# Encoder layer with attention, convolution and experts on one core: x tiles over two queues, convolution parts in place, a new list order, router products behind the last chunk

## What is computed

```python
h = rms_norm(x, norm1_g)
u = h @ w_in                                   # 1024 x 2560
q, k, v, uc = split(u)                         # 3 x 512, 1024
a = neighbourhood_attention(q, k, v, rpb)      # 8 heads x 64
c = conformer_conv(uc)                         # GLU, depthwise conv of width 31, layer norm, swish
x = x + concat(rms_norm(a), rms_norm(c)) @ w_out
h = rms_norm(x, norm2_g)
x = x + hier_moe(h)                            # top group of 4, then top 2 of its 8 experts
y = rms_norm(x, final_g)
```

## Time and profile before

| what | us |
|---|---|
| median of 3 runs | 912.96 |
| lowest, highest | 912.54, 914.18 |
| the profiled execution's own time | 913.56 |
| its span, first to last instruction | 911.7 |

### The profile page before, as it was taken

One profiled execution on the slowest core, in us unless ns is written; L12 is line 12 of the kernel. 1 busy time (PEld: TensorE's weight loads), 2 busy tenths in 40 slices (PEclk: granted clock), 3 DMA queues, 4 the chain that ended last, 5 costly groups with the idle time before them and its releaser, 6 DMA issues.

```text
span 911.7 us, 15694 instructions
## 1 busy us (share of the span) xinstructions
PE 848.1 (93%) x5814; PEld 571.5 (63%) x5815; DVE 374.4 (41%) x697; ACT 242.3 (27%) x482; POOL 139.2 (15%) x288
## 2 busy tenths in 40 slices
PE   3989999999979999989999879999999999999984
PEld 2879977777757878965555445555555555555531
DVE  5399979796374535541111101111111111111146
ACT  5223216545675222101111111111111111111122
POOL 4200010000000001022222111212222212121113
PEclk9998999999979999899999999999999999999997
DMA  7543543413251293959999999999999999999975
GB/s 210 125 91 104 156 162 139 151 47 105 66 166 47 104 401 147 402 214 418 423 418 420 419 419 422 418 420 420 420 420 419 420 420 420 419 414 420 391 290 185
DMA packets 82014, 266.04 MB, mean 292 GB/s; under 512 B 19129, under 2 KB 44985, under 8 KB 57401
## 3 DMA queue, kind: packets, MB, share of 16 engines
q1 hardware_dynamic: 64272, 245.11, 68.9%
q0 software_dynamic: 7888, 18.78, 5.4%
q10 hardware_dynamic: 9816, 1.66, 1.0%
HBM read 247.53 MB, written 27.34 MB: 302 GB/s over the span
## 4 chain that ended last, share of the span: by engine, by line
PE 55%; DMA 16%; SPq 7%; DVE 6%; issue 1%; ACT 1%; POOL 0%; POOLq 0%; DVEq 0%; ACTq 0%
DMA big<-in_w_up 16%; PE ps L1299 14%; PE ps L1336 9%; PE ps L1053 8%; PE ps L1186 7%; SPq L771 7%; PE ps L1302 3%; PE ps L1314 2%; DVE big L1713 2%; PE ps L1290 2%; PE ps L1072 2%; PE ps L1105 1%; PE ps L1084 1%; PE ps L690 1%; PE ps L1205 1%
## 5 line engine op out<-in xcount | busy, mean ns | idle before, releaser
L2026 DVE TENSOR_TENSOR big<-ps,big 64x256 f32<-64x256 f32 x78 | 33.2, 426 | 392.0 <-ACT big L1592 392.0
L1302 PE MATMUL ps<-ring,big 128*64 128x256 f32 x704 | 156.1, 379 | 4.7 <-DMA ring<-in_w_up 4.7
L1299 PE MATMUL ps<-ring,big 128*64 128x256 f32 x704 | 156.4, 379 | 0.9 <-DVE big L2015 0.9
L1053 PE MATMUL ps<-hT,w_split 128*128 128x512 f32 (+1 forms) x768 | 145.7, 345 | 4.1 <-DVE hT L1651 3.6
L1053 PEld LDWEIGHTS ps<-hT,w_split 128*128 128x128 f32 x768 | 118.6, 191 | 26.2 <-issue 11.7
L1299 PEld LDWEIGHTS ps<-ring,big 128*64 128x64 f32 x704 | 96.0, 137 | 56.3 <-issue 12.5
L1302 PE MATMUL ps<-big 128*64 128x256 f32 x544 | 121.5, 380 | 5.1 <-DMA big<-in_w_up 5.1
L1299 PE MATMUL ps<-big 128*64 128x256 f32 x544 | 121.6, 380 | 0.0
L1302 PEld LDWEIGHTS ps<-ring,big 128*64 128x64 f32 x704 | 96.1, 137 | 10.5 <-DMA ring<-in_w_up 6.4
L1299 PEld LDWEIGHTS ps<-big 128*64 128x64 f32 x544 | 73.9, 137 | 39.2 <-issue 9.0
L1592 ACT ACTIVATE big<-ps 64x256 f32<-64x256 f32 x78 | 29.3, 375 | 245.1 <-PE ps L1302 231.7
(11 more groups left out here) (244 smaller groups left out, 1092.5 us busy)
## 6 DMA issues: line engine op xcount, KB each, us to landing
ring<-in_w_gate SPq DMA_DIRECT2D x44, 1024.0 KB, 27.3
ring<-in_w_up SPq DMA_DIRECT2D x44, 1024.0 KB, 28.0
ring<-in_w_down SPq DMA_DIRECT2D x44, 1024.0 KB
big<-in_w_gate SPq DMA_DIRECT2D x20, 1024.0 KB
big<-in_w_up SPq DMA_DIRECT2D x20, 1024.0 KB
big<-in_w_down SPq DMA_DIRECT2D x20, 1024.0 KB
w_raw<-in_w_in SPq DMA_DIRECT2D x20, 512.0 KB, 4.1
results<-spare POOLq DMA_DIRECT2D x12, 512.0 KB, 2.9
```

The source lines that it names most:

```text
L1053: mm = pe.matmul(ps[:, n % 2, 0:size], w_split[:, sub, hi_w, k, :], hT[:, k // 4, hi_h, k % 4, cols], **flags)
L1299: pe.matmul(ps[0:BLK, 6 * h, 0:FH], xT[:, k % (KD // 2), q, :], gate_w[s][:, k, fs], start=(k == 0), stop=(k == KD - 1))
L1302: mm = pe.matmul(ps[BLK:2 * BLK, 6 * h + 1, 0:FH], xT[:, k % (KD // 2), q, :], up_w[s][:, k, fs], start=(k == 0), stop=(k == KD - 1))
L2026: nc.vector.tensor_tensor(hb[:, fs], ps[BLK:2 * BLK, 6 * h + 1, 0:FH], sG[:, fs], ALU.mult).then_inc(hb_ready[h], 1)
```

## The change

- **Start:** SyncE loads x tiles 0 and 3, n1 and the weights; ScalarE's queue loads tiles 1, 2, 4 and 5. The orders of ScalarE and VectorE over squares, scaling and parts are rewritten. The very first group is cut by columns: its first half needs h tiles 0 and 1 only.
- **Convolution parts in place:** high and low part of the convolution get buffers of their own (conv_hi, conv_lo), so they no longer wait for hT. w_out block 1 has its own raw and split buffers, too.
- **List order:** CHUNKS has conv 3 ahead of qk 0; COST, FIRST, PATIENCE are new numbers for plan().
- **Second norm and scores of the router:** the turned tiles use other banks (TURN_BANK), the router products move, fillers are fewer.
- **Rows stored once:** h_rows has half its size; row_idx holds its own indices, from one more comparison and one addition.
- **First expert round on TensorE** is written out, with the first block's register loads ahead of the wait for its rows.

```diff
-CHUNKS = [("conv", 0), ("conv", 1), ("v", 0), ("v", 1), ("conv", 2), ("qk", 0), ("conv", 3), ("qk", 1), ("qk", 2), ("qk", 3)]
+CHUNKS = [('conv', 0), ('conv', 1), ('v', 0), ('v', 1), ('conv', 2), ('conv', 3), ('qk', 0), ('qk', 1), ('qk', 2), ('qk', 3)]
...
-    return 4 if CHUNKS[c][0] != "v" and g % 2 == 0 else 2
+    return 4 if CHUNKS[c][0] != "v" and g % 2 == 0 and (c, g) != (0, 0) else 2
...
-FIRST = dict(win=50, ht=1, sc=10, tn=8, va=8, inv=7, mean=15, meanb=3, var=2, rows=0, rowsb=0, ssc=3, asum=6, poa=45, po=45, tnh=20, lgt=2,
+FIRST = dict(win=22, ht=26, sc=8, tn=5, va=14, inv=6, mean=16, meanb=16, var=19, rows=2, rowsb=18, ssc=0, asum=19, poa=23, po=23, tnh=-5, lgt=26,
...
+TURN_BANK = (4, 0, 4, 0, 4, 2)
...
-        in_line(("chi", j), [("silu", j), last_group])
+        in_line(("chi", j), [("silu", j), ("ssc",)])
...
-            after += [("alo", PAIRS - 1), ("sh", ASLOTS - 1)] if s else [("clo", JC - 1)] + [taker(*g) for g in groups[-2:]]
+            after += [("alo", PAIRS - 1), ("sh", ASLOTS - 1)] if s else [("clo", JC // 2 - 1)] + [taker(*g) for g in groups[-2:]]
...
-        in_line(("po", s), [], line="po")
+        in_line(("po", s), [] if s else [("clo", JC - 1)], line="po")
...
-    h_rows = nc.dram_tensor("h_rows", (4 * T, D // 2), F32, kind="Internal").ap()
+    h_rows = nc.dram_tensor("h_rows", (2 * T, D // 2), F32, kind="Internal").ap()
...
-            for t in range(NT):
-                sp.dma_start(x[:, t, :], rows_of(x_prompt, x_sample, t)).then_inc(x_in[t], 16)
-                if t == 0:
-                    sp.dma_start(n1, bass.AP(norm1.tensor, 0, [[0, P], [1, D]])).then_inc(n1_in, 16)
-                elif t == NTS - 1:
-                    load_win(0)
+            sp.dma_start(x[:, 0, :], rows_of(x_prompt, x_sample, 0)).then_inc(x_in[0], 16)
+            sp.dma_start(n1, bass.AP(norm1.tensor, 0, [[0, P], [1, D]])).then_inc(n1_in, 16)
+            sp.dma_start(x[:, 3, :], rows_of(x_prompt, x_sample, 3)).then_inc(x_in[3], 16)
+            load_win(0)
             load_win(1)
...
+            sp.wait_ge(osplit_done, OUT_CHUNKS - 1)
             sp.wait_ge(wout_done, NT * OUT_CHUNKS // 2)
...
             for t in range(NT):
                 sp.wait_ge(h2_ready, t + 1)
-                for j in range(2):
-                    sp.dma_start(h_whole[j * T + t * P:j * T + (t + 1) * P, :], h2[:, t, :]).then_inc(h2_out, 16)
+                sp.dma_start(h_whole[t * P:(t + 1) * P, :], h2[:, t, :]).then_inc(h2_out, 16)
...
+                if n == 0:
+
+                    pe.wait_ge(h_ready, 2 * q + 2)
+                    some = slice(2 * P * q, 2 * P * (q + 1))
+                    for k in range(KD):
+                        for m, (hi_w, hi_h) in enumerate(HI_LO):
+                            mm = pe.matmul(ps[:, 0, some], w_split[:, 0, hi_w, k, :], hT[:, k // 4, hi_h, k % 4, some],
+                                           start=(k == 0 and m == 0), stop=(k == KD - 1 and m == 2))
...
-                    if a[0] == NT - 1:
-                        pe.wait_ge(x2_done, max(g for g in range(len(OUT)) if OUT_BANK[g] == 7) + 1)
-                        stay_busy(4)
...
-            stay_busy(32)
+            pe.wait_ge(x2_done, len(OUT))
+            stay_busy(26)
             pe.wait_ge(order_ready, 1)
...
             pe.wait_ge(table_ready, 1)
+            first_blocks = blocks_of(0)
             pe.wait_ge(xb_copied, 1)
             turn_rows()
             stay_busy(3)
...
+            for t in (1, 2, 4, 5):
+                act.dma_start(x[:, t, :], rows_of(x_prompt, x_sample, t)).then_inc(x_in[t], 16)
...
             def hi_of_conv(j):
                 act.wait_ge(silu_done, j + 1)
-                nc.scalar.activation(mT[:, 0, 0, j, :], conv_out[:, j, :], ACT.Copy,
+                if j == 0:
+                    act.wait_ge(ssc_done, 1)
+                nc.scalar.activation(conv_hi[:, j, :], conv_out[:, j, :], ACT.Copy,
                                      scale=vec[:, V_GO + JC + j:V_GO + JC + j + 1]).then_inc(chi_done, 1)
...
             def lo_of_w_out(n):
                 dve.wait_ge(ohi_done, n + 1)
+                if n == 0:
+                    dve.wait_ge(win_done, len(GROUP_AT))
...
             link(V.tensor_scalar(nobody[:], ps[:, 5, 0:NB], 0.0, float(8 * T), ALU.is_equal, ALU.mult))
+            link(V.tensor_scalar(second, ps[:, 5, 0:NB], float(2 * T), float(-2 * T), ALU.is_gt, ALU.mult))
+            link(V.tensor_tensor(second, second, nobody[:], ALU.add))
```

More of the change, by code:

```diff
@@ L196, in parts @@
                 after += [taker(*groups[n - 2])] if n >= 2 else []
-            in_line(("win", c, g, q), after, COST["narrow" if kind == "v" or g % 2 else "part"], "win")
-            if n == 0 and q < 2:
-                in_line(("ht", 4 + q), [], line="win")
+            in_line(("win", c, g, q), after, COST["first" if n == 0 else "narrow" if kind == "v" or g % 2 else "part"], "win")
+            if n == 0 and q == 0:
+                for t in range(NTS, NT):
+                    in_line(("ht", t), [], line="win")
         done = ("win", c, g, parts_of(c, g) - 1)
@@ L333, in release @@
     def release(name):
-        engine, at = ENGINE[name[0]], 5.0 if name[0] == "strip" else 0.0
+        engine, at = ENGINE[name[0]], 8.0 if name[0] == "strip" else 0.0
         for d in work[name][1]:
@@ L1027, in turn_h @@
                 mm.then_inc(xps, 1)
-            for t in range(4):
+            for t in range(NTS):
                 turn_h(t)
@@ L1339, in expert_block, with blocks_of, blocks, expert @@
                 mm.then_inc(y_done, 1)
+            def blocks_of(place):
+                n = pe.value_load(table[0:1, bass.ds(place, 1)], min_val=1, max_val=MAXN)
+                first = pe.value_load(table[0:1, bass.ds(place + E, 1)], min_val=0, max_val=MAXB - 1)
+                return n, first
+            def blocks(n, first, s, target):
+                with pe.Fori(0, n) as j:
+                    expert_block(first + j, s, target)
+            def expert(place, s, target):
+                blocks(*blocks_of(place), s, target)
             pe.wait_ge(table_ready, 1)
+            first_blocks = blocks_of(0)
             pe.wait_ge(xb_copied, 1)
@@ L1344, in _ @@
             stay_busy(3)
-            def expert(place, s, target):
-                n = pe.value_load(table[0:1, bass.ds(place, 1)], min_val=1, max_val=MAXN)
-                first = pe.value_load(table[0:1, bass.ds(place + E, 1)], min_val=0, max_val=MAXB - 1)
-                with pe.Fori(0, n) as j:
-                    expert_block(first + j, s, target)
-            with pe.Fori(0, E // SLOTS) as i:
+            blocks(*first_blocks, 0, 16)
+            for place in range(1, SLOTS):
+                expert(place, place, 16)
+            with pe.Fori(1, E // SLOTS) as i:
                 for s in range(SLOTS):
@@ L1656, in lo_of_run @@
                 nc.vector.tensor_tensor(lo, w_raw[:, run % 2], fp32(hi), ALU.subtract).then_inc(split_done, 1)
-            scaled(0)
-            scaled(1)
-            for t in range(NT):
-                lo_of_h(t)
-                if t + 2 < NT:
-                    scaled(t + 2)
-                if t in (2, 4):
-                    lo_of_run(t // 2 - 1)
+            for t in range(3):
+                scaled(t)
+            lo_of_h(0)
+            scaled(3)
+            lo_of_h(1)
+            lo_of_run(0)
+            lo_of_h(2)
+            scaled(4)
+            lo_of_h(3)
+            scaled(5)
+            lo_of_run(1)
+            lo_of_h(4)
+            lo_of_h(5)
             dve.wait_ge(vec_in, 16)
```

113 lines of the change are left out of this document (63 added, 50 removed).

## The result

| | before | after |
|---|---|---|
| median, us | 912.83 (4 runs) | 903.86 (4 runs) |
| lowest, highest | 912.54, 914.18 | 901.84, 905.35 |
| the profiled execution's own time | 913.56 | 904.92 |
| its span | 911.7 | 903.1 |

The change makes the kernel 1.1% faster: the ratio is 0.9893, with a 95% interval of 0.9876 to 0.991. That is 9.0 us by the medians and 8.6 between the two profiled executions, where 15.2 were forecast.

A forecast was written before the change was run, and what follows sets the result against it. Ahead of 399 us TensorE bounds the kernel; the expert stage behind is a fixed block of some 481 us. Terms -2.5 - 7.1 - 6.9 - 1.2 + 2.5 = -15.2 us gave 897.8 us, range 890 to 907.

The forecast's parts named there:

- Term 1: At the start: reordered squares, splits and a column-cut first group bring TensorE's w_in products earlier, -2.5 us.
- Rival B: At the start: norm row and tile 3 come late, the term becomes +1, total 901.3 us; chance 0.08.
- Term 2: At the convolution's end: parts in their own place remove a stall and half clock, less new waits, -7.1 us.
- Term 3: Around the last output chunk: three of six groups of router products move behind it, at full clock, -6.9 us.
- Term 4: At the list: fewer fillers, two more VectorE operations, register loads moved ahead of the wait, -1.2 us.
- Term 5: At the first gather: weight preloads still fill the DMA engines, so the gather takes longer, +2.5 us.
- A: Before the expert stage: VectorE binds in part, its waits and half clock cost 6 us, total 904; chance 0.15.
- E: Conv-and-attention stretch: VectorE becomes its bound, the moved chunk's 28 us of taps join the path, total 926; chance 0.05.
- F: At the expert stage's start: everything won ahead is given back as a wait, total 913; chance 0.03.

The follow-up runs named there:

- experiment 4: Kernel after with all six x tiles and the norm row on SyncE's one queue, new orders kept: 903.44 us, ratio 0.9902.
- experiment 2: Kernel after with the remaining weight preloads issued behind the third stored tile instead of the sixth: 898.94 us, ratio 0.9842.
- experiment 5: Three edits of the kernel after: first, high parts wait for the last w_in group again, 902.39 us; old chunk sequence, 911.3 us; both, 909.29 us.
- experiment 6: Kernel before with only the chunk sequence changed (conv 3 ahead of qk 0), planned with its old numbers: 920.4 us, ratio 1.0057.
- experiment 8: Kernel of experiment 2 with the first three groups of router products placed late among the output products: 897.65 us, ratio 0.9826.
- experiment 7: Kernel after with the router products of the first three tiles back between the output products: 904.64 us, ratio 0.9903.
- experiment 1: Kernel after with 16 fillers instead of 4 ahead of the wait for the first gathered rows: 901.22 us, ratio 0.9869.

## Why the prediction was right, and where it was not

The forecast was 897.8 with 890 to 907; the time is 903.86, inside. The sign and the places were right; the sum was 6 us too good, and the mechanism behind its largest term was wrong for the most part. The first expert product stood at 388.66, not at 384. That the time lies inside the range owes something to the range's width: no term names what took most of the 6 us.

**Term 1 (forecast -2.5):** measured -4.2 in the profile, and 2.7 to 4.3 over the nine kernels with this start (the wait ends at 62.59 to 64.27, against 66.92). The norm row came late, as feared (VectorE's first scaling waited for it until 11.29), but TensorE begins on w_in at 21.74, and with one queue at 21.06. Rival B was right that the row lands late (9.7 us for 6.1) and wrong on the price. The rule of the Trainium skill (DMA: Bandwidth & Descriptors, Issuing engines are not separate DMA queues) that transfers started by several engines run on the same 16 DMA engines agrees with experiment 4: the gain of the two queues is nil. The estimate tied to it, -1.5 for the reordering, was too small.

**Term 2 (forecast -7.1):** the size was right where the clock held, the cause was wrong. From the wait at chunk 1 to the last output product TensorE takes 230.1 us (110.95 to 341.09), where it took 242.7 (115.75 to 358.45): 12.6 less, forecast 15.1 for terms 2 and 3 together (7.1, and 8.0 ahead of the last chunk). In the profile of experiment 2, whose clock holds in 105 to 165, it is 227.1 (111.83 to 338.91): 15.6 less. The wait for the split of w_out was 0.80 (0.5), the one at mean 2 2.37 (1.5), the one at mean 3 didn't come. But the step "After the change the convolution's parts have a place of their own and no longer wait for the last w_in group" doesn't carry the 7.1: experiment 5 puts that wait back, which costs 1.4 us up to the last output product and nothing in the total. The sequence of chunks, which the prediction had only as a cost, is worth 7.4 us in the changed kernel (experiment 5). It does not take the stretch away alone: in the kernel before, with the old numbers, stretch and half clock stay (experiment 6). So the gain belongs to the sequence together with the planner's new numbers, and the place has a small part in it.

**Term 3 (forecast -6.9):** the part ahead of the last chunk (-8.0) is in the numbers of term 2. Behind that chunk it took 16.5 us where 13.3 were forecast, against 12.2 before. The step that failed is "13.3 us from the last chunk to the last router product at full clock". The 13.3 were worked out with products at full clock, but a row of nothing but router products and turns had a mean of 0.79: 3.2 us more. The price at full clock was right: 8.04 us for half the router products in experiment 8, and three groups of 1.7 more make 13.1. The row is at 0.79 or 0.80 in six profiles, at 0.89 in the two with the wait put back, and with half as many router products at 1.00 (7 and 8).

**Term 4 (forecast -1.2):** right where the clock holds. Last router product to first order product 7.6 us for 8.5; the next steps to the gather's issue 14.6 (365.17 to 379.79) for 14.0. The 0.8 of the register loads is in experiment 2 (2.0 for 2.87), and in the kernel after it is hidden by half clock (2.97).

**Term 5 (forecast +2.5):** measured +2.9, and experiment 2 shows its cause. What the forecast lacked is what stands behind it: TensorE has fillers for a gather of 3 us, a longer one lets it stand 3.26 us, and the turn and the first block then run at half clock. In the profile 0.9 us more stand ahead of the first expert product and 1.8 behind than forecast; experiment 1's 12 fillers take away 0.95 and 1.15 of them, so 0.6 of the 2.7 is not shown to be clock.

**The sum in the profile:** -15.2, +3.2 clock in the router products, +2.7 behind the gather (2.1 of it clock), +0.4 gather, +2.5 ahead of the last chunk (mostly the half clock of that execution at the two means), -1.7 start, -0.6 between the start and chunk 1's mean (48.2 us for 48.8, in no term): -8.7, against -8.6 measured. Of the rivals, A gave the nearest number (904), and part of its mechanism was there: VectorE's waits were 1.2 us over the forecast (0.80 and 2.37 for 0.5 and 1.5), and half clock followed them in this profile. But most of the 6 us came from elsewhere. What was priced wrongly was TensorE's clock: in a row where it does not wait, and behind waits that term 5 and the two means made. E and F fell: TensorE is busy 102.64 of 105.00 us from 136.20 to 241.20, and the expert stage is 480.94 us.

## What to carry to other kernels

A transfer made longer is paid twice if the engine behind it was kept busy for the old length: once in the wait, once in the clock of the work that follows. When a stall goes away after a change of several parts, put each part back alone before naming it, and look at its stage as well as the total: here the wait put back cost 1.4 us in its stage and nothing in the total, and the sequence that the gain hung on made the old kernel slower. And spread narrow products between wide ones rather than into one row, provided that each stands where its input is long ready; here that held the clock, but its gain in time (1.3 us) is not told apart from nothing, and it moved the preloads closer to the gather.

## What the runs showed of the hardware that was not expected

- TensorE fell to its lower clock while it was busy without a gap: 16.51 of 16.51 us with products of 36 columns and turns, mean clock 0.79; three groups of the same router products between output products of 512 columns ran at 1.00 (experiment 8, 327.76 to 341.29). In two other profiles the same row of instructions had 0.89.
- The same instructions with the same two waits of 2.4 us (105 to 165 us) had a mean clock of 0.94 in two profiles (the kernel after, experiment 8), 0.97 in experiment 7's, and 1.00 in four (experiments 1, 2, 4 and the first of 5); runs of the kernel after spread over 3.5 us (901.84 to 905.35).
- Six x tiles through one queue or two gave the same start: the value chunk's wait ends at 62.65 with one, and at 62.59 to 64.27 with two.
